# Fused two-block transformer pass: the first norm and its modulation as a pipeline over chunks, and the embedding product of the gated per-layer embedding ahead of its gate

## Chip, cores and metric

The kernel runs on one NeuronCore of a Trainium2 chip. The metric is the device time of one execution in microseconds (us), median over executions. Engines are named as the profile names them: PE (TensorE, matrix products; PEld its weight loads), DVE (VectorE), ACT (ScalarE), POOL (GpSimd), SP (SyncE, which issues nearly all DMAs).

## What is computed

A sequence of 512 tokens of width 1024 goes through two blocks. Only the places that the change touches are spelled out; the rest (differential attention, native sparse attention, two squared-ReLU MLPs, an mLSTM layer, a dilated window attention) is unchanged.

```python
# first block: conditioning by a vector c, layer 0
c_act = silu(c)                                      # (1, 1024)
mod = c_act @ ada_w[layer] + ada_b[layer]            # six rows of 1024
sh_a, sc_a, gt_a, sh_m, sc_m, gt_m = split(mod, 6)
h = rms_norm(x, attn_norm[layer]) * (1 + sc_a) + sh_a
mix = diff_attention(h, a_w_in, ...)                 # starts with h @ a_w_in (1024 x 3072)

# second block: per-layer embedding, once after the mLSTM layer, once at the very end
def ple_add(h, p_l, norm_g, w_gate, w_proj):
    gate = sigmoid(rms_norm_2(h, norm_g) @ w_gate)   # 1024 x 1024
    return h + (p_l @ w_proj) * gate                 # p_l: 512 x 256, w_proj: 256 x 1024
```

## The kernel before

Activations stand transposed in SBUF: `x` is 8 chunks (KC = 8) of 128 features by 512 tokens. All large weights come as one stream of halves of 128 x 2048 fp32 (1 MB) in the order of `STREAM`. Half n lands in slot n % 2 of `raw` (`load_half`, L600, issued by SP); ACT copies it rounded into `wH` (`hi`, L393), DVE writes the remainder `wL = raw - wH` (`lo`, L398). Activations are split in the same way into `hH` and `hL`. Each product of a 128 x 128 weight block with 512 tokens is three matmuls (`three`, L412 to L414). A tile of the output is four blocks of 128 rows in four PSUM banks and takes two halves and 96 matmuls (`tile_mm`); tile a uses banks 4 * (a % 2) onward.

A norm has three parts. `sq_act` (L485) squares the chunks, `sq_dve` (L493) adds the first seven up, `stats_pe` (L502, L505) multiplies by a matrix of 1/1024, which puts the mean on all partitions, and `rstd_act` (L509, L511) makes the inverse root. `apply_dve` and `apply_act` then make for each chunk the product tmp = x * scale * rstd (L515, DVE), hH (L549 or L551, ACT) and hL (L521 or L524, DVE).

Nothing is scheduled by a planner: each engine runs its own list (`act_first`, `dve_first`, ..., `pe_fourth`) in the order written, and semaphores tie them. An instruction that waits holds up all that stands behind it on its engine; this goes for SP's DMA issues too.

The first stage: SP loads c (broadcast), x, then 16 blocks of the modulation matrix as four transfers of 2 MB (`ada_h`), then halves 0 and 1 of the first weight, the relative-bias table `bt` (4 MB, by way of a row in DRAM) and, in the loop, one half and up to three further modulation blocks (`ada_load`, L593) a turn. DVE makes silu from ACT's exp(-c) with an addition, a reciprocal and a product (L1187 to L1191), adds up the squares, then takes the 16 dot products of modulation rows (`ada_sum`, L582: one pass over 128 x 1024 each), two small column operations (`mod_cols`, `mod_scale`), and applies the norm. PE runs the first tile after that.

The gated embedding (`ple_pe`, `ple_act`, `ple_dve`, L2297 to L2355): PE makes the two gate tiles (a, a + 1), then the product of the embedding with its weight (a + 2, a + 3), whose weight is a half of the stream, after them. ACT takes the sigmoid of the gate (L2308), DVE multiplies and adds to x (L2333, L2323). After the first use the next norm follows, after the second the output is stored (L2788). Before the last use, `dve_fourth` runs `lo` of the two first gate halves and only then the residual additions of the layer before (L2847 to L2850).

## Time and profile before

| | |
|---|---|
| median of 3 runs | 2163.93 us (2160.59 to 2164.48) |
| profiled execution | 2160.12 us, its span 2158.3 us |
| busy PE / PEld | 1986.0 us (92%) / 1634.8 us (76%) |
| busy DVE / ACT / POOL | 1173.3 us (54%) / 839.1 us (39%) / 0.2 us (0%) |
| mean granted TensorE clock | 0.953 of full speed |
| DMA | 223.85 MB, mean 104 GB/s |

The span runs from the first to the last instruction of the profiled execution. A row of the timeline gives start, length and engine, and in brackets how long the engine had been idle and what ended that. Lengths of matmuls overlap, since they are pipelined, so distances between starts are the better measure. A row of a window gives busy time and count of instructions for each engine, then the granted clock.

### The profile page before, as it was taken

The page shows a single profiled execution, that of the slowest core. Times are in us where ns is not written, and L with a number is a line of the kernel's source. Part 1 is how long each engine was busy: PE and PEld are TensorE (multiplying, and loading weights), DVE is VectorE, ACT ScalarE, POOL GpSimd, SP SyncE. Part 2 cuts the span into 40 slices and gives each one's busy share as a digit, 9 for nine tenths or more (in the row PEclk, how much of TensorE's full clock was granted, in tenths as well). Part 3 has the DMA queues.
Part 4 walks back from the last instruction along what each step waited for, and adds up shares of the span by engine and source line. Part 5 has one row for each costly group of instructions (what it writes and reads, how often), then busy time and mean ns, then how long its engine had stood idle before and what let it go on. Part 6 is the DMA issues. An engine that isn't in the chain of part 4 may idle for free.

```text
span 2158.3 us, 24312 instructions
## 1 busy us (share of the span) xinstructions
PE 1986.0 (92%) x9298; PEld 1634.8 (76%) x9298; DVE 1173.3 (54%) x2046; ACT 839.1 (39%) x1303; POOL 0.2 (0%) x4
## 2 busy tenths in 40 slices
PE   1999979999998998889899999997999999999969
PEld 0877658888886786889878888885878877777857
DVE  8557756565666375556544343436634554646553
ACT  3226624132233532356633132234344443556432
POOL 0000000000000000000000000000000000000000
PEclk9999999999999978699999999998999999999989
DMA  9551064565654221000022222221222132131021
GB/s 357 203 198 40 1 216 158 173 214 175 210 179 136 98 84 53 1 1 2 6 104 98 98 97 97 97 97 42 95 78 79 40 135 85 59 137 59 1 88 59
DMA packets 42216, 223.85 MB, mean 104 GB/s; under 512 B 4444, under 2 KB 5212, under 8 KB 23694
## 3 DMA queue, kind: packets, MB, share of 16 engines
q1 hardware_dynamic: 41602, 222.25, 29.4%
q8 instruction: 56, 0.92, 0.2%
q10 hardware_dynamic: 524, 0.41, 0.1%
q14 instruction: 34, 0.28, 0.0%
HBM read 219.45 MB, written 3.19 MB: 103 GB/s over the span
## 4 chain that ended last, share of the span: by engine, by line
PE 83%; DVE 8%; DMA 3%; ACT 3%; issue 2%; SPq 0%; DVEq 0%; ACTq 0%
PE bank L412 23%; PE bank L413 22%; PE bank L414 22%; PE bank L1487 3%; PE bank L1458 2%; DMA raw<-wts_d 1%; DMA adab<-ada_d 1%; PE bank L1448 1%; PE bank L2568 1%; PE bank L1449 1%; DMA ada<-ada_d 1%; DVE tmp L515 1%; ACT wH L393 1%; DVE wL L398 1%; PE bank L676 1%
## 5 line engine op out<-in xcount | busy, mean ns | idle before, releaser
L412 PE MATMUL bank<-hH,wH 128*128 128x512 f32 x1344 | 539.0, 401 | 68.2 <-DVE hL L524 36.9
L413 PE MATMUL bank<-hL,wH 128*128 128x512 f32 x1344 | 533.6, 397 | 0.0
L414 PE MATMUL bank<-hH,wL 128*128 128x512 f32 x1344 | 532.7, 396 | 0.0
L412 PEld LDWEIGHTS bank<-hH,wH 128*128 128x128 f32 x1344 | 258.9, 193 | 133.4 <-issue 70.1
L398 DVE TENSOR_TENSOR wL<-raw,wH 128x2048 fp32r<-128x2048 f32 x78 | 178.6, 2290 | 291.0 <-ACT wH L393 290.8
L941 ACT ACTIVATE wH<-raw 128x2048 fp32r<-128x2048 f32 x64 | 122.7, 1917 | 470.5 <-PE bank L414 470.5
L413 PEld LDWEIGHTS bank<-hL,wH 128*128 128x128 f32 x1344 | 259.1, 193 | 54.5 <-issue 1.0
L414 PEld LDWEIGHTS bank<-hH,wL 128*128 128x128 f32 x1344 | 258.5, 192 | 55.2
L393 ACT ACTIVATE wH<-raw 128x2048 fp32r<-128x2048 f32 x78 | 149.1, 1912 | 317.4 <-PE bank L414 281.7
L979 DVE TENSOR_TENSOR wL<-raw,wH 128x2048 fp32r<-128x2048 f32 x64 | 146.6, 2290 | 230.7 <-ACT wH L941 230.6
L414 PE MATMUL bank<-aH,wL 128*128 128x512 f32 x512 | 199.4, 389 | 0.0
L413 PE MATMUL bank<-aL,wH 128*128 128x512 f32 x512 | 199.4, 389 | 0.0
L412 PE MATMUL bank<-aH,wH 128*128 128x512 f32 x512 | 199.4, 389 | 0.0
L582 DVE CUSTOM_DVE_ANT_0 adab<-adab,cb 128x1024 f32<-128x1024 f32 x96 | 115.4, 1223 | 88.9 <-DMA adab<-ada_d 88.9
L412 PE MATMUL bank<-wH,hH 128*128 128x512 f32 x320 | 132.7, 415 | 2.4 <-ACT kT L1162 1.7
L414 PE MATMUL bank<-wH,hL 128*128 128x512 f32 x320 | 126.2, 394 | 0.0
L413 PE MATMUL bank<-wL,hH 128*128 128x512 f32 x320 | 126.1, 394 | 0.0
L412 PEld LDWEIGHTS bank<-aH,wH 128*128 128x128 f32 x512 | 96.1, 188 | 20.0
L414 PEld LDWEIGHTS bank<-aH,wL 128*128 128x128 f32 x512 | 96.1, 188 | 19.9
L413 PEld LDWEIGHTS bank<-aL,wH 128*128 128x128 f32 x512 | 96.1, 188 | 19.8
L1487 PEld LDWEIGHTS bank<-vB,ptB 128*128 128x128 f32 x640 | 90.3, 206 | 17.9 <-issue 5.7
L1549 DVE CUSTOM_DVE_ANT_0 sB<-bank,bt 128x128 f32<-128x128 f32 (+3 forms) x128 | 59.3, 488 | 75.8 <-PE bank L1449 75.1
(321 smaller groups left out, 2568.1 us busy)
## 6 DMA issues: line engine op xcount, KB each, us to landing
raw<-wts_d SPq DMA_DIRECT2D x142, 1024.0 KB, 4.9
adab<-ada_d SPq DMA_DIRECT2D x96, 512.0 KB, 4.3
ada<-ada_d SPq DMA_DIRECT2D x4, 2048.0 KB, 22.3
bt<-bias_rows SPq DMA_DIRECT2D x1, 4096.0 KB, 12.9
x<-x_d SPq DMA_DIRECT2D x1, 2048.0 KB, 9.6
out_d<-x SPq DMA_DIRECT2D x4, 512.0 KB, 2.7
pF<-p_d SPq DMA_DIRECT2D x2, 512.0 KB, 3.7
values_by_token<-vD SPq DMA_DIRECT2D x1, 1024.0 KB, 4.3
```

The lines of the kernel that those rows point to most:

```text
L393: act.activation(wH[:, n % 2, :], raw[:, n % 2, :], ACT.Copy).then_inc(w_hi, 1)
L398: dve.tensor_tensor(wL[:, n % 2, :], raw[:, n % 2, :], wH[:, n % 2, :].bitcast(F32), ALU.subtract).then_inc(w_lo, 1)
L412: pe.matmul(o, l[0], r[0], start=start, stop=False)
L413: pe.matmul(o, l[0], r[1], start=False, stop=False)
L414: return pe.matmul(o, l[1], r[0], start=False, stop=stop)
L515: dve.scalar_tensor_tensor(out=tmp[:, c % 3, :], in0=x[:, c, :], scalar=scale(c), in1=rstd[:, :], op0=ALU.mult, op1=ALU.mult).then_inc(tmp ...
L582: return dve.tensor_tensor_reduce(slot, slot, sb["cb"][:, :], 1.0, 0.0, ALU.mult, ALU.add, dst)
L941: act.activation(wH[:, n % 2, :], raw[:, n % 2, :], ACT.Copy).then_inc(w_hi, 1)
L979: dve.tensor_tensor(wL[:, n % 2, :], raw[:, n % 2, :], wH[:, n % 2, :].bitcast(F32), ALU.subtract).then_inc(w_lo, 1)
L1458: last = pe.transpose(bank[:, 2 + u % 2, j * P:(j + 1) * P], pB[:, u % 2, j * P:(j + 1) * P], ident[:, :])
L1487: last = pe.matmul(o[:, r * (HD + 1):(r + 1) * (HD + 1)], ptB[:, u % 2, part.start + j * P:part.start + (j + 1) * P], vB[:, j, b * GRP + g ...
L1549: dve.tensor_tensor_reduce(sB[:, u % 2, part], bank[:, u % 2, part], sb["bt"][:, 4 * g + r, T - w:T], -SCALE, BIG, ALU.add, ALU.min, nm[:, ...
```

## The change

First stage. ACT takes a sigmoid by table instead of the exponential and DVE multiplies it with c, so the addition and the reciprocal go; ACT loads one more table set after the sigmoid. The weight half 0 is loaded ahead of x. The 16 modulation blocks come as eight pairs (a shift block and its scale block, 1 MB) in four slots; a pair's two dot products start from the bias and gain columns, so that they give the finished shift and scale of one chunk. DVE makes for each chunk the two dot products and the norm's product, ACT writes hH and the shifted value, and POOL subtracts to hL. The table `bt` is no longer issued ahead of the loop over weight halves but in it, behind halves 2 to 4 and the modulation blocks 18 to 23, and half 5 stands behind it.

Gated embedding. Its weight leaves the stream and is loaded with p into the `bias` region (`peF`), split there (`ple_split_act`, `ple_split_dve`). PE makes chunks 0 and 1 of the product before the norm's statistics, 2 and 3 after them, 4 to 7 between the two gate tiles; ACT copies them to `pp`. The second gate tile comes last, its second half bank by bank. In the fourth part the residual additions now come ahead of `lo` of the first gate half, and `lo` of the second moves into the apply. After the first use three squares and sums of the next norm move.

```diff
         def sp_first(sp):
             sp.dma_start(sb["cb"][:, :], d["c"].to_broadcast([P, D])).then_inc(cb_back, 16)
+            load_half(sp, 0)
             sp.dma_start(x[:, :, :], d["x"]).then_inc(x_in, 16)
-            for g in range(4):
...
+            for c in range(KC):
+                if c >= 4:
+                    sp.wait_ge(ada_pre, 2 * (c - 4) + 2)
+                sp.dma_start(ada_pair(c), pairs[c]).then_inc(ada_h[c % 4], 16)
+                if c == 2:
                     load_half(sp, 1)
...
+            load_half(sp, 2)
+            for k in range(2):
+                ada_load(sp, 16 + k)
             sp.wait_ge(f_row, 2)
             sp.dma_start(fscr, sb["frow"][:, :]).then_inc(f_out, 16)
...
-            for n in range(12):
+            for n in range(1, 12):
                 load_half(sp, n + 2)
-                for k in range(max(3 * n - 1, 0), min(3 * n + 2, 24)):
+                for k in range(3 * n - 1, min(3 * n + 2, 24)):
                     ada_load(sp, 16 + k)
+                if n == 2:
+                    sp.wait_ge(f_out, 16)
+                    sp.dma_start(sb["bt"][:, :, :], skewed).then_inc(bt_in, 16)
...
-            act.activation(sb["ce"][:, :], sb["cb"][:, :], ACT.Exp, scale=-1.0).then_inc(first_e, 1)
+            act.activation(sb["ce"][:, :], sb["cb"][:, :], ACT.Sigmoid).then_inc(first_e, 1)
+            act.preload_act_table_set(EXP_LN)
...
-            apply_act(act, 0, lambda c: mod(c))
+            for c in range(KC):
+                act.wait_ge(tmp_done, c + 1)
+                t = tmp[:, c % 3, :]
+                act.activation(hH[:, c, :], t, ACT.Identity, bias=mod(c))
+                act.activation(t, t, ACT.Identity, bias=mod(c)).then_inc(h_hi, 1)
+                if c == 1:
+                    hi(act, 1)
...
+            def pair_sums(c):
+                dve.wait_ge(ada_h[c % 4], 16 * (c // 4 + 1))
+                a = ada_pair(c)
+                dve.tensor_tensor_reduce(a[:, 0, :], a[:, 0, :], cb, 1.0, col("ada_b", c), ALU.mult, ALU.add,
+                                         mod(c)).then_inc(ada_pre, 1)
+                dve.tensor_tensor_reduce(a[:, 1, :], a[:, 1, :], cb, col("attn_norm", c), start[:, c:c + 1],
+                                         ALU.mult, ALU.add, mod(8 + c)).then_inc(ada_pre, 1)
...
+            for c in range(KC):
+                pair_sums(c)
+                dve.wait_ge(ada_pre, 2 * c + 2)
+                if c == 0:
+                    dve.wait_ge(rstd_done, 1)
+                if c >= 3:
+                    dve.wait_ge(h_lo, c - 2)
+                dve.scalar_tensor_tensor(out=tmp[:, c % 3, :], in0=x[:, c, :], scalar=mod(8 + c), in1=rstd[:, :],
+                                         op0=ALU.mult, op1=ALU.mult).then_inc(tmp_done, 1)
+                if c == 2:
+                    lo(dve, 1)
...
+        @block.gpsimd
+        def _(pool):
+            for c in range(KC):
+                pool.wait_ge(h_hi, c + 1)
+                pool.tensor_tensor(hL[:, c, :], tmp[:, c % 3, :], hH[:, c, :].bitcast(F32), ALU.subtract)\
+                    .then_inc(h_lo, 1)
...
         def ple_act(act, l, a, n):
             act.preload_act_table_set("sigmoid_and_others")
+            ple_product_act(act, l, a, 0)
+            hi(act, n + 2)
+            act.wait_ge(half_used, n + 2)
+            for m in range(4):
+                o, freed = evac(act, a + 2, m)
+                act.activation(sg[:, m, :], o, ACT.Sigmoid).then_inc(freed, 1)
+            ple_product_act(act, l, a, 1)
+            hi(act, n + 3)
+            if n + 4 < N_HALF:
+                hi(act, n + 4)
+            for m in range(4):
+                o, freed = evac(act, a + 3, m)
+                bank_done(act, DONE0[a + 3], m, n + 4)
+                act.activation(sg[:, 4 + m, :], o, ACT.Sigmoid).then_inc(freed, 1)
+                if l == 0 and m < 3:
+                    sq_act(act, 7, lambda e, c: e.wait_ge(ple_x, c + 1), [m])
+            if n + 4 < N_HALF:
+                act.preload_act_table_set(EXP_LN)
...
+            for c in range(4, KC):
+                gated(c)
+                if l == 0 and 5 <= c:
+                    sq_dve(dve, 7, [c - 4])
+                grow(c)
...
         def dve_fourth(dve):
+            sq_dve(dve, 7, range(4, 7))
...
             d_dve(dve)
-            lo(dve, N_DO + 2)
-            lo(dve, N_DO + 3)
+            ple_split_dve(dve, 1)
             dve.wait_ge(half_used, N_DO + 1)
             residual_dve(dve, 67, 0, None)
+            lo(dve, N_DO + 2)
             sq_dve(dve, 8, [1, 2, 3])
             second_tile(dve, 8, 68, None, N_DO + 2)
-            apply_dve(dve, 9, 8, lambda c: col("ple_norm", 8 + c), None)
+            apply_dve(dve, 9, 8, lambda c: col("ple_norm", 8 + c), None, lambda e: lo(e, N_DO + 3))
             ple_dve(dve, 1, 69, N_G1)
...
             last.then_inc(half_used, 1)
+            ple_product_pe(pe, 1, 69, (0, 1))
             stats_pe(pe, 8, 69)
+            ple_product_pe(pe, 1, 69, (2, 3))
             ple_pe(pe, 1, 69, N_G1, 72)
```

The order on DVE in the first stage, after the sums of squares: `ada_62` is the buffer of modulation blocks, the dot product is an `ISA` row with its accumulator read behind it. Before, from the last blocks to the norm's products:

```order
L582 ISA ada_63,mods<-ada_63,cb 128x1024
L582 ISA mods 128x1
L398 TENSOR_TENSOR wL<-raw,wH 128x2048
L1079 TENSOR_TENSOR mods<-mods,cols 128x16
L1086 SCALAR_TENSOR_TENSOR mods<-mods,cols 128x8
L515 SCALAR_TENSOR_TENSOR tmp<-x,mods,rstd 128x512 x3
L524 SCALAR_TENSOR_TENSOR hL<-tmp,mods,hH 128x512
```

and in the changed kernel, chunks 0 and 1:

```order
L496 TENSOR_TENSOR tmp<-tmp 128x512 x6
L1223 ISA ada_62,mods<-ada_62,cb,cols 128x1024
L1223 ISA mods 128x1
L1225 ISA ada_62,mods<-ada_62,cb,rs,cols 128x1024
L1225 ISA mods 128x1
L1236 SCALAR_TENSOR_TENSOR tmp<-x,mods,rstd 128x512
L1223 ISA ada_62,mods<-ada_62,cb,cols 128x1024
```

The norm's product stands behind two dot products instead of sixteen, and the rows for hL are gone from DVE.

The order on DVE in the fourth part, from the last row of the attention on. Before:

```order
L2694 TENSOR_TENSOR hL<-qD,hH 128x512
L398 TENSOR_TENSOR wL<-raw,wH 128x2048 x2
L574 TENSOR_TENSOR x<-bank,x 128x512 x4
L493 TENSOR_TENSOR tmp<-tmp 128x512 x3
L574 TENSOR_TENSOR x<-bank,x 128x512 x2
```

and in the changed kernel:

```order
L2776 TENSOR_TENSOR hL<-qD,hH 128x512
L2335 TENSOR_TENSOR pL<-pF,pH 128x1024
L2337 TENSOR_TENSOR peL<-peF,peH 128x2048
L577 TENSOR_TENSOR x<-bank,x 128x512 x4
L401 TENSOR_TENSOR wL<-raw,wH 128x2048
L496 TENSOR_TENSOR tmp<-tmp 128x512 x3
L577 TENSOR_TENSOR x<-bank,x 128x512 x2
```

The four residual additions stand behind the two splits of the embedding instead of behind two weight splits.

## Rows read from the trace of the kernel before

**Rows 1.** Timeline of PE, first stage: start, us, [idle before it <- who ended that]

```profile
20.00 2.05 PE L502 MATMUL bank<-tmp,mean 128*128 128x512 f32 x2 [20.00 <-DVE tmp L493]
...
49.85 0.77 PE L412 MATMUL bank<-hH,wH 128*128 128x512 f32 x1 [23.86 <-DVE hL L524]
```

**Rows 2.** The chain that ended last, first stage: start, us

```profile
22.19 13.42 DMA raw<-wts_d
```

**Rows 3.** Timeline of DVE, first stage

```profile
15.19 4.67 DVE L493 TENSOR_TENSOR tmp<-tmp 128x512 f32<-128x512 f32 x6
...
20.91 1.22 DVE L582 CUSTOM_DVE_ANT_0 ada<-ada,cb 128x1024 f32<-128x1024 f32 x1
...
22.06 1.22 DVE L582 CUSTOM_DVE_ANT_0 ada<-ada,cb 128x1024 f32<-128x1024 f32 x1
...
37.57 2.29 DVE L398 TENSOR_TENSOR wL<-raw,wH 128x2048 fp32r<-128x2048 f32 x1 [3.00 <-ACT wH L393]
...
46.97 2.08 DVE L515 SCALAR_TENSOR_TENSOR tmp<-x,mods,rstd 128x512 f32<-128x512 f32 x3
```

**Rows 4.** Timeline of ACT, first stage

```profile
10.75 1.67 ACT L485 ACTIVATE tmp<-x 128x512 f32<-128x512 f32 x3 [4.17 <-DMA x<-x_d]
...
23.79 0.69 ACT L509 ACTIVATE rstd<-bank,one 128x512 f32<-128x512 f32 x1 [4.01 <-PE bank L505]
...
50.53 0.72 ACT L551 ACTIVATE hH<-tmp,mods 128x512 fp32r<-128x512 f32 x1 [0.73 <-DVE tmp L515]
```

**Rows 5.** DMA issues, 0 to 120 us: KB each, median us to landing

```profile
bt<-bias_rows SPq DMA_DIRECT2D x1, 4096.0 KB, 12.9
```

**Rows 6.** DMA issues, 2060 to 2100 us

```profile
raw<-wts_d SPq DMA_DIRECT2D x2, 1024.0 KB, 4.9
```

**Rows 7.** Timeline of ACT: the first instruction after the fourth tile

```profile
138.62 2.06 ACT L1162 ACTIVATE kT<-bank 128x512 f32<-128x512 f32 x4 [8.90 <-PE bank L414]
```

**Rows 8.** Timeline of PE around the first gated embedding

```profile
1762.71 1.02 PE L502 MATMUL bank<-tmp,mean 128*128 128x512 f32 x2
...
1769.69 0.70 PE L412 MATMUL bank<-hH,wH 128*128 128x512 f32 x1 [4.25 <-DVE hL L521]
...
1827.96 1.10 PE L502 MATMUL bank<-tmp,mean 128*128 128x512 f32 x2 [2.01 <-DVE tmp L493]
...
1837.16 0.47 PE L412 MATMUL bank<-hH,wH 128*128 128x512 f32 x1 [4.25 <-DVE hL L521]
```

**Rows 9.** Timeline of ACT after the first gated embedding

```profile
1819.05 1.28 ACT L2310 ACT_TABLE_LOAD   x1
```

**Rows 10.** Windows: length, busy of PE, PEld, DVE, ACT, POOL, then granted clock

```profile
2096.70:2100.50 3.80, 3.79 (x9) 3.03 (x10) 3.73 (x6) 1.60 (x3) 0.00 (x0) 0.50 0.00 0
2100.50:2104.00 3.50, 3.50 (x16) 2.84 (x16) 3.43 (x6) 1.97 (x4) 0.00 (x0) 0.95 0.02 5
```

**Rows 11.** Timeline of SP, DVE and PE ahead of the last gated embedding

```profile
2058.10 0.33 SPq L2784 DMA_DIRECT2D pF<-p_d  x1
...
2077.70 2.29 DVE L398 TENSOR_TENSOR wL<-raw,wH 128x2048 fp32r<-128x2048 f32 x1 [8.58 <-ACT wH L393]
2079.91 2.48 DVE L574 TENSOR_TENSOR x<-bank,x 128x512 f32<-128x512 f32 x4
...
2088.71 2.04 PE L502 MATMUL bank<-tmp,mean 128*128 128x512 f32 x2 [13.05 <-DVE tmp L493]
2090.55 1.92 PE L505 MATMUL bank<-tmp,mean 128*128 128x512 f32 x2
...
2096.71 0.77 PE L412 MATMUL bank<-hH,wH 128*128 128x512 f32 x1 [4.24 <-DVE hL L521]
```

**Rows 12.** The end: last matmul, sigmoids, last additions, stores

```profile
2142.47 2.07 ACT L2308 ACTIVATE sg<-bank 128x512 f32<-128x512 f32 x4 [8.90 <-PE bank L414]
2152.92 0.39 PE L414 MATMUL bank<-pH,wL 128*128 128x512 f32 x1
2153.95 1.28 DVE L2323 TENSOR_TENSOR x<-x,sg 128x512 f32<-128x512 f32 x2
```

More of the change, by code:

```diff
@@ L308, in place @@
     t("sg", [P, KC, T], "hid")
+    t("pp", [P, KC, T], "hid", 16 * K)
+    t("peF", [P, HALF], "bias")
+    t("peH", [P, HALF], "bias", 8 * K, F32R)
+    t("peL", [P, HALF], "bias", 16 * K, F32R)
     t("pF", [P, 2, T], "misc")
@@ L466, in program @@
         sq_sum = sem("sq_sum")
-        SUMMED = [4 if s == 7 else 7 for s in range(9)]
+        SUMMED = [7] * 9
         SUM0 = [sum(SUMMED[:s]) - s for s in range(9)]
@@ new lines, in dve_first @@
+            start = rs[:, 16:24]
+            dve.scalar_tensor_tensor(out=start, in0=cols[:, COL0["ada_b"] + 8:COL0["ada_b"] + 16], scalar=1.0,
+                                     in1=cols[:, COL0["attn_norm"]:COL0["attn_norm"] + KC], op0=ALU.add,
+                                     op1=ALU.mult).then_inc(cb_ready, 1)
+            dve.wait_ge(first_e, 2)
+            dve.tensor_tensor(one[:, 2:3], cc[:, 0, 3:4], cc[:, 0, 2:3], ALU.subtract).then_inc(lam_s, 1)
+            dve.wait_ge(lam_s, 3)
@@ L2290, in m_core_dve, with ple_load @@
                 rest(c, c - 4)
[L2293 to L2295 removed]
+        p_in, p_hi, p_lo, ple_x, ple_mm, ple_g = (sem(n) for n in (
+            "p_in", "p_hi", "p_lo", "ple_x", "ple_mm", "ple_g"))
+        sg, pF, pH, pL, pp = (sb[n] for n in ("sg", "pF", "pH", "pL", "pp"))
+        peF, peH, peL = sb["peF"], sb["peH"], sb["peL"]
+        def ple_load(sp, l):
+            sp.dma_start(pF[:, :, :], d["p"][l]).then_inc(p_in, 16)
+            sp.dma_start(peF[:, :], d["ple"][l]).then_inc(p_in, 16)
@@ new lines, in ple_split_act, with ple_split_dve @@
+        def ple_split_act(act, l):
+            act.wait_ge(p_in, 32 * (l + 1))
+            act.activation(pH[:, :, :], pF[:, :, :], ACT.Copy).then_inc(p_hi, 1)
+            act.activation(peH[:, :], peF[:, :], ACT.Copy).then_inc(p_hi, 1)
+        def ple_split_dve(dve, l):
+            dve.wait_ge(p_hi, 2 * l + 1)
+            dve.tensor_tensor(pL[:, :, :], pF[:, :, :], pH[:, :, :].bitcast(F32), ALU.subtract).then_inc(p_lo, 1)
+            dve.wait_ge(p_hi, 2 * l + 2)
+            dve.tensor_tensor(peL[:, :], peF[:, :], peH[:, :].bitcast(F32), ALU.subtract).then_inc(p_lo, 1)
@@ new lines, in ple_product_pe @@
+        def ple_product_pe(pe, l, a, chunks):
+            pe.wait_ge(p_lo, 2 * l + 2)
+            for c in chunks:
+                if c < 4:
+                    pe.wait_ge(acc_free[0], 4 * ((a - 1) // 2) + c + 1)
+                else:
+                    pe.wait_ge(acc_free[1], 4 * (a // 2) + c - 4 + 1)
+                for k in range(2):
+                    w = slice(k * D + c * P, k * D + (c + 1) * P)
+                    last = three(pe, bank[:, c % 4, :], (peH[:, w], peL[:, w]), (pH[:, k, :], pL[:, k, :]),
+                                 k == 0, k == 1)
+                last.then_inc(ple_mm, 1)
@@ L2309, in ple_act @@
-            if n + 6 < N_HALF:
+            ple_product_act(act, l, a, 0)
[8 more added lines that the diff above has]
+                hi(act, n + 4)
+            for m in range(4):
+                o, freed = evac(act, a + 3, m)
[3 more added lines that the diff above has]
+                    sq_act(act, 7, lambda e, c: e.wait_ge(ple_x, c + 1), [m])
@@ L2338, in ple_dve @@
[L2338 to L2355 removed]
+            lo(dve, n + 2)
@@ new lines, in ple_dve, with block @@
+            gated(0)
+            for c in range(1, 4):
+                gated(c)
+                grow(c - 1)
+            grow(3)
+            lo(dve, n + 3)
+            if n + 4 < N_HALF:
+                lo(dve, n + 4)
+            for c in range(4, KC):
+                gated(c)
+                if l == 0 and 5 <= c:
+                    sq_dve(dve, 7, [c - 4])
+                grow(c)
+        def ple_pe(pe, l, a, n, hbase):
+            def block(t, j, kk, m):
+                k = 4 * j + kk
+                return three(pe, bank[:, 4 * (1 - t) + m, :], wpart((n + 2 * t + j) % 2, kk, m * P, P),
+                             (hH[:, k, :], hL[:, k, :]), k == 0, k == KC - 1)
+            acc_wait(pe, a)
+            for j in range(2):
+                pe.wait_ge(w_lo, n + j + 1)
+                for kk in range(4):
+                    pe.wait_ge(h_lo, hbase + 4 * j + kk + 1)
+                    for m in range(4):
+                        last = block(0, j, kk, m)
+                last.then_inc(half_used, 1)
+            ple_product_pe(pe, l, a, range(4, KC))
+            pe.wait_ge(w_lo, n + 3)
+            for kk in range(4):
+                for m in range(4):
+                    if kk == 0:
+                        pe.wait_ge(acc_free[0], 4 * ((a + 1) // 2) + m + 1)
+                    last = block(1, 0, kk, m)
+            last.then_inc(half_used, 1)
+            pe.wait_ge(w_lo, n + 4)
+            for m in range(4):
+                for kk in range(4):
+                    last = block(1, 1, kk, m)
+                last.then_inc(m_done if m < 3 else half_used, 1)
```

161 lines of the change are left out of this document (50 added, 111 removed).

## Prediction

> **What bounds the kernel now.** PE is busy for 92% of the span, so time can come only from stretches in which it stands still, or from work taken off it. I read first what PE waits for at the start: 20.0 us for the sums of squares and 23.86 us for the first hL, so that its first tile begins at 49.85 [rows 1]. The chain that ended last tells what is behind the second wait: a transfer, the first weight half, queued behind 8 MB of modulation blocks and landed at 35.6 us [rows 2]. The timelines of DVE and ACT give the prices, the DMA issues those of transfers, and PE's rows around the two gated embeddings show three more gaps: 4.25 us ahead of the first gate, 2.0 and 4.25 us after it [rows 8], and 13.05 and 4.24 us ahead of the last [rows 11].
>
> **Prices.** A matmul at full clock starts every 0.22 to 0.23 us (16 in 3.5 us), at the lower level of 1.2 GHz 9 take 3.8 us [rows 10]. I use 0.227: 2.72 us for the 12 matmuls of one chunk, 10.9 for a half, 21.8 for a tile, 1.36 for one chunk of the embedding product (6). A spell at the low level ahead of a tile costs 3.8 - 9 x 0.227 = 1.8 us. A dot product takes 1.15 us (22.06 - 20.91), `lo` 2.2 with the hand-over, ACT's rounding ahead of it 1.9 (landed at 35.6 [rows 2], `lo` begins at 37.57), a norm's product 2.08 / 3 = 0.69 [rows 3], hH 0.7 [rows 4]. 4 MB land 12.9 us after issue [rows 5], 1 MB 4.9 us [rows 6]: 2.67 us for each MB and 2.2 us fixed.
>
> **Start, up to the first tile.** The silu by table saves nothing by itself: the squares wait for x, landed at 10.75 [rows 4], and the dot products for their blocks. Half 0 ahead of x costs 1 MB, so x lands at 13.4 and the six sums, which took from 15.2 to 19.9 since DVE was still at the silu, now run from about 15.0 to 19.5. The statistics and the root take what they took (19.9 to 25.2: Ln begins at 23.8 and takes 0.69, the Exp after it as much [rows 4]), so rstd is there at 24.7. Pair 0 (4.5 MB in all) lands at about 16 and is summed by 22. From 24.7 DVE sets the pace: per chunk 2 x 1.15 + 0.69 + 0.1 for semaphores = 3.1 us, above PE's 2.72. With `lo` of half 1 and its wait (2.5) the eighth product ends at 24.7 + 0.7 + 7 x 3.1 + 2.5 = 49.6. Pairs 4 to 7 are issued when their slots come free; the last, at about 35, lands at 40 and is wanted at 46, so they are hidden. hH and the shifted value take 1.4 us.
>
> The subtraction on POOL has no row. Its nearest row is the same operation on DVE, 0.6 to 0.7 us, from below; from above I take the DVE price of a subtraction four times as wide, 2.29 us. I take 1.2, nearer the lower end, since the operation and size are those of the lower row and only the engine differs. Then the last chunk is ready at 49.6 + 1.4 + 1.2 = 52.2 and the tile ends at 54.9. It ended at 49.85 + 21.8 + 1.4 (its first matmuls were slow) = 73.0: **18.1 us** less.
>
> **What is late next.** Tile 1 wants `lo` of half 2, behind the eighth apply: 49.6 + 1.4 + 1.9 (ACT) + 2.2 = 55.1, 0.2 us lost. Then the queue. `bt` went out before PE had begun; now SP issues it after modulation block 23, which waits for the sum of block 21, at about 70 us (54.9 and from there two halves' turns on DVE, each `lo` and three dot products whose blocks come 3.5 us after their slots are free). Half 5 is issued behind it: (4 + 1) x 2.67 + 2.2 = 15.6 us, landing at 86; block 24, next in the queue, at 87.6. On DVE the sum of block 24 stands ahead of `lo` of half 5: 87.6 + 1.15 + 2.2 = 91.1. PE wants it at 55.1 + 3 x 10.9 = 87.8. I count a **new wait of 3.3 us**. Bounds: 0, if the queue lets the small transfers through, and 6 with a slower `bt`. From there the loop has its old slack. The fourth tile, which ended at 138.5 [rows 7], ends at 55.1 + 65.3 + 3.3 = 123.7. **Start: -14.8 us.**
>
> **First gated embedding.** Chunks 0 and 1 of the product, 2.7 us, stand ahead of the statistics, which began at 1762.71 with no gap [rows 8]. A part of these 2.7 us was a wait for the eighth square, so statistics end 1.95 us later; the gate starts at 1771.6 instead of 1769.7. Chunks 2 and 3 lie in the 4.25 us gap. With only 1.7 us of it left I expect no spell at the low clock: -1.8 us (bounds 0 and -1.8). Chunks 4 to 7 cost 5.4 us between the tiles. The second tile ends at 1771.6 + 21.8 + 5.4 + 21.8 = 1820.6; before, the product ended at 1825.8. What follows is worse than before: ACT has the last sigmoid (0.5 us), a table load (1.28) [rows 9] and only then square 3, and DVE's `sq_dve` of chunk 3 stands ahead of the last addition to x. Counting on at 0.64 us a step (1.28 / 2) [rows 12] (square 3, sum 3, addition, then sums 4 to 6, each fed by a square) the sum is complete 6.1 us after the tile's end, and PE, idle so long, makes the statistics at the low clock in 3.8 us (2088.71 to 2090.55 + 1.9) [rows 11] instead of about 2. The next tile starts 4.25 us later, at 1820.6 + 6.1 + 3.8 + 4.25 = 1834.8 against 1837.16: **-2.4 us** (bounds -0.6 and -4.2 by the two clock terms). The splits added ahead of that (1.2 + 2.3 us on DVE) stand with four residual additions (2.5 us) [rows 11] in front of `lo` of a half that PE wants 10.9 us before 1762.7, at 1751.8: its slot is free at 1740.9, and 1740.9 + 2.5 + 3.5 + 2.2 = 1749.1. They cost nothing, with 2.7 us of cover.
>
> **Last gated embedding.** The 13 us gap came from `lo` of the second gate half (2077.7), which had to wait for PE to free its slot and stood ahead of the residual additions (2079.9) [rows 11]. Now DVE has ahead of them only the splits. p is issued at 2058.1; with its weight behind it, 1.5 MB, they land at 2058.1 + 0.4 + 4.0 + 2.2 = 2064.4 or so. ACT (1.9) rounds the weight by 2066.3, DVE is through with the remainder at 2068.6. The additions and sums took 8.7 us from 2079.9 to the start of the statistics; with one `lo` (2.2) among them: 2068.6 + 8.7 + 2.2 = 2079.5 instead of 2088.7, 9.2 us. Chunks 0 and 1 of the product fill PE's wait, so it stays warm and the statistics take 2.1 instead of 3.8 us, another 1.7; the gate starts at 2079.5 + 2.1 + 4.24 = 2085.8, 10.9 us earlier, and without the slow spell (1.8). Chunks 0 to 3 lie in gaps: 5.4 us less behind the gate. The end is a sigmoid longer: 0.5 + 0.69 + 0.68 with the hand-overs, 2.3 us after the last matmul against 2.1 [rows 12]. **-10.9 - 1.8 - 5.4 + 0.2 = -17.9 us**; without the clock term -16.1.
>
> **Sum.** -14.8 - 2.4 - 17.9 = -35.1 us. The profiled execution took 2160.12 us and would take 2125.0. The median, 2163.93, is 3.8 us above it, and gives 2128.8. I forecast 2128.8 for the median.
>
> **Rivals.**
> 1. *POOL's subtraction holds DVE up.* It becomes ready while DVE is in the second dot product; if the two engines exclude each other, POOL starts at its end and the norm's product, on the path, waits for it: its length less 0.1 us, seven times. With 1.2 us: +7.7, **2136.5**; with 0.69 and 2.29: +4 and +15. For it: DVE is the bottleneck there and its rows are back to back. Against it: no row shows POOL and DVE together at all. The Trainium skill states just this rule (SBUF — State Buffer, "Who interferes with whom"): a DVE instruction with two SBUF inputs and a GpSimd instruction that reads SBUF lock each other out of a shared read interface for the whole instruction. No run here shows it yet. The skill's GPSIMD Engine Reference (3.1) has a two-input operation on GpSimd 1.96 times as long as on VectorE, which would make an estimate of 1.35 us of the 0.69 row, and with it the lock would cost 8.8 us.
> 2. *`bt` hides.* If queue and loop have more slack than I count, the 3.3 us are not lost: **2125.5**.
> 3. *The embedding's weight is late.* In the fourth part everything I gain begins with peL at 2068.6. If the 1 MB lands 10 us late, the 9.2 us go: **2138.0**. Against it: DMA moves little there.
> 4. *Slower than before: POOL sets the pace.* The product of chunk c waits for hL of chunk c - 3. Once a subtraction takes more than 3.1 us the chain runs at POOL's pace and the tile ends near 29.5 + 8 x its length. The other parts bring 20.3 us and the waits behind the tile take 3.5, so against 73.0 the total turns positive at a tile end of 89.8, a subtraction of 7.5 us; at 8.5 us it ends at 97.5 and the time is **2171.6**. That is nearly four times my upper row.
> 5. *Nothing moves:* the gaps close but the waits turn up again one stage later, 2164. The stages after the first tiles are bound by PE, which speaks against it.
>
> **How the numbers follow.** Forecast 0.47, rival 1 0.33, rival 2 0.10, rival 3 0.05, rival 4 0.02, rival 5 0.03. The forecast's own range is 2121 to 2133: 3.8 us for where the median falls, 3.6 for the two clock terms of 1.8. With rivals 1 to 3 and the middle of the bounds of POOL the range is 2119 to 2142. A measurement of this kernel tells about 0.2%, 4.3 us, from no change: faster 0.95, same 0.03, slower 0.02.
>
> **What would show it.** Right: first hL product on PE near 28 us, DVE's norm products 3.1 us apart, the fourth tile's evacuation near 124 us with one PE wait for `lo` of about 4 us behind `bt`; PE's longest wait ahead of the last gate about 1 us; the last matmul 2.3 us ahead of the last addition. Rival 1 shows in DVE's rows about 4.2 us apart, with POOL's rows in the holes. Wrong would be: a wait of PE above 5 us in the fourth part, a POOL row above 3 us, or waits for weights in tiles 1 and 2.

## Result and profile after

| | before | after |
|---|---|---|
| median | 2164.2 us (2160.59 to 2164.86, 4 runs) | 2149.43 us (2146.22 to 2151.21, 4 runs) |
| profiled execution, its span | 2160.12 us, 2158.3 us | 2151.21 us, 2149.4 us |
| busy PE / DVE / ACT / POOL | 1986.0 / 1173.3 / 839.1 / 0.2 us | 1991.0 / 1169.8 / 853.0 / 16.3 us |
| mean granted TensorE clock | 0.953 | 0.946 |

The ratio is 0.9933, 95% interval 0.9916 to 0.9951: 14.8 us faster by the medians, faster by more than the 0.2% that can be told. The forecast was 2128.8 us with a range of 2119 to 2142: too low by 20.6 us, and the measured time lies above the range. The two profiled executions lie at opposite ends of their sets (before's is its fastest, after's its slowest), so their spans differ by 8.9 us only. I therefore read the traces stage by stage, each against a landmark just ahead of it, and come back at the end to what lies between the stretches.

| stretch | before | after | forecast | measured |
|---|---|---|---|---|
| span's start to the fourth tile's evacuation (ACT, kT) | 138.62 | 140.39 | -14.8 | **+1.8** |
| ACT's table load ahead of the second m_out tile, to the first product of kv2 | 1726.95 to 1837.16: 110.21 | 1733.47 to 1843.55: 110.08 | -2.4 | **-0.1** |
| issue of `pF` for the last embedding, to the span's end | 2058.10 to 2158.3: 100.2 | 2066.21 to 2149.4: 83.2 | -17.9 | **-17.0** |

The page's busy line of the changed kernel:

```profile
PE 1991.0 (93%) x9292; PEld 1635.7 (76%) x9292; DVE 1169.8 (54%) x2038; ACT 853.0 (40%) x1328; POOL 16.3 (1%) x12
```

Most of the miss, 16.6 us, is in the table's first row. PE's first tile begins at 34.52 us, 15.3 us earlier than in [rows 1], where 28 was forecast:

```profile
25.06 2.04 PE L505 MATMUL bank<-tmp,mean 128*128 128x512 f32 x2 [25.06 <-DVE tmp L496]
...
34.52 0.77 PE L415 MATMUL bank<-hH,wH 128*128 128x512 f32 x1 [4.81 <-POOL hL L3004]
```

DVE's timeline of the first stage after the change (rows as in [rows 3]):

```profile
6.69 1.23 DVE L1201 TENSOR_TENSOR cb<-cb,ce 128x1024 f32<-128x1024 f32 x1 [5.39 <-ACT ce L1147]
15.60 0.22 DVE L1205 CUSTOM_DVE_ANT_0 lamb<-lamb 128x64 f32<-128x64 f32 x1 [7.68 <-DMA lamb<-lam_d]
...
18.04 2.29 DVE L401 TENSOR_TENSOR wL<-raw,wH 128x2048 fp32r<-128x2048 f32 x1 [1.39 <-ACT wH L396]
20.25 4.66 DVE L496 TENSOR_TENSOR tmp<-tmp 128x512 f32<-128x512 f32 x6
...
30.04 0.75 DVE L1236 SCALAR_TENSOR_TENSOR tmp<-x,mods,rstd 128x512 f32<-128x512 f32 x1 [2.65 <-ACT rstd L514]
30.71 1.28 DVE L1223 CUSTOM_DVE_ANT_0 ada<-ada,cb,cols 128x1024 f32<-128x1024 f32 x1
...
31.91 1.34 DVE L1225 CUSTOM_DVE_ANT_0 ada<-ada,cb,rs 128x1024 f32<-128x1024 f32 x1
...
33.30 1.62 DVE L1236 SCALAR_TENSOR_TENSOR tmp<-x,mods,rstd 128x512 f32<-128x512 f32 x1
34.84 1.27 DVE L1223 CUSTOM_DVE_ANT_0 ada<-ada,cb,cols 128x1024 f32<-128x1024 f32 x1
...
36.05 1.33 DVE L1225 CUSTOM_DVE_ANT_0 ada<-ada,cb,rs 128x1024 f32<-128x1024 f32 x1
...
37.43 1.65 DVE L1236 SCALAR_TENSOR_TENSOR tmp<-x,mods,rstd 128x512 f32<-128x512 f32 x1
...
41.20 2.30 DVE L1223 CUSTOM_DVE_ANT_0 ada<-ada,cb,cols 128x1024 f32<-128x1024 f32 x1
...
44.81 0.75 DVE L1236 SCALAR_TENSOR_TENSOR tmp<-x,mods,rstd 128x512 f32<-128x512 f32 x1
...
60.50 1.63 DVE L1236 SCALAR_TENSOR_TENSOR tmp<-x,mods,rstd 128x512 f32<-128x512 f32 x1
```

Two things are to be seen. DVE stood still for 7.68 us, until 15.60. Its wait is for all five small transfers of ACT's queue, and the profile names the broadcast lambda rows (`lamb`) as the last to land. The sums of squares began at 20.25 instead of the forecast 15.0 and the first product at 30.04 instead of 24.7. And the products are 4.13 us apart (33.30 to 37.43), not 3.1: six of the eight show 1.62 to 1.66 us, but the first and the fourth (44.81), which have no POOL work beside them, 0.75. Ahead of the fourth, the dot product at 41.20 has POOL's third subtraction (40.52 to 42.41) beside it and takes 2.30 us where the others take 1.28. POOL's timeline of the same stretch:

```profile
32.24 2.14 POOL L3004 TENSOR_TENSOR hL<-tmp,hH 128x512 fp32r<-128x512 f32 x1 [31.79 <-ACT tmp L1163]
36.37 2.16 POOL L3004 TENSOR_TENSOR hL<-tmp,hH 128x512 fp32r<-128x512 f32 x1 [1.99 <-ACT tmp L1163]
...
63.57 1.29 POOL L3004 TENSOR_TENSOR hL<-tmp,hH 128x512 fp32r<-128x512 f32 x1 [2.00 <-ACT tmp L1163]
```

The last subtraction, with DVE idle beside it, takes 1.29 us; the others 1.89 to 2.17. The second row shows what happens. It starts at 36.37 while DVE's dot product runs (36.05 to 37.38) and ends at 38.53, which is the dot product's end plus 1.15; DVE's product starts at 37.43 and ends 0.55 us after POOL. Each waits for the other inside its own row.

The third place is the third tile, which takes the weight halves 4 and 5 (counted from zero it is tile 2; the expectation of `bt_early` below calls it tile 1). SP's timeline and the DMA issues (KB, median us to landing; 12.9 in [rows 5]), then the timelines of DVE and PE, then windows (length; busy PE, PEld, DVE, ACT, POOL; granted clock), all of the changed kernel:

```profile
82.58 0.43 SPq L1128 DMA_DIRECT2D bt<-bias_rows  x1
83.06 4.83 SPq L603 DMA_DIRECT2D raw<-wts_d  x1
```

```profile
bt<-bias_rows SPq DMA_DIRECT2D x1, 4096.0 KB, 15.2
```

```profile
101.59 1.23 DVE L585 CUSTOM_DVE_ANT_0 adab<-adab,cb 128x1024 f32<-128x1024 f32 x1 [14.48 <-DMA adab<-ada_d]
...
102.74 2.28 DVE L401 TENSOR_TENSOR wL<-raw,wH 128x2048 fp32r<-128x2048 f32 x1
```

```profile
105.08 0.79 PE L415 MATMUL bank<-hH,wH 128*128 128x512 f32 x1 [4.46 <-DVE wL L401]
```

```profile
98.00:102.00 4.00, 2.62 (x12) 1.84 (x10) 0.41 (x1) 1.67 (x1) 0.00 (x0) 1.00 0.75 301
102.00:106.00 4.00, 0.92 (x2) 0.83 (x3) 4.00 (x4) 2.19 (x5) 0.00 (x0) 0.65 0.55 184
106.00:110.00 4.00, 4.00 (x11) 3.03 (x11) 1.40 (x4) 1.17 (x1) 0.00 (x0) 0.50 0.98 381
```

On DVE the `lo` of half 5 stands behind the dot product of a modulation block that landed only at 101.6 us, 19.0 us after the issue of `bt`. PE waits 4.46 us, and then the granted clock is at 0.50, the 1.2 GHz level, with 11 matmuls in 4 us. The forecast had the wait, at 3.3 us, and no low clock behind it.

Ahead of the first embedding PE waited for a weight half (first row below); behind it the statistics took 3.7 us, the low-clock length, as forecast:

```profile
1749.36 0.47 PE L415 MATMUL bank<-hH,wH 128*128 128x512 f32 x1 [2.00 <-DVE wL L401]
...
1835.56 2.05 PE L505 MATMUL bank<-tmp,mean 128*128 128x512 f32 x2 [6.24 <-DVE tmp L496]
1837.40 1.92 PE L508 MATMUL bank<-tmp,mean 128*128 128x512 f32 x2
1843.55 0.76 PE L415 MATMUL bank<-hH,wH 128*128 128x512 f32 x1 [4.24 <-DVE hL L524]
```

PE around the last embedding, beside [rows 11], with the waits of 13.05 and 4.24 us down to 1.20, 0.40 and 1.49:

```profile
2084.99 0.47 PE L415 MATMUL bank<-pH,peH 128*128 128x512 f32 x1 [1.20 <-DVE x L577]
...
2088.37 1.10 PE L505 MATMUL bank<-tmp,mean 128*128 128x512 f32 x2 [0.40 <-DVE tmp L496]
...
2094.91 0.47 PE L415 MATMUL bank<-hH,wH 128*128 128x512 f32 x1 [1.49 <-DVE hL L524]
```

### The profile page after: what moved, and what is told of

Read it like the earlier page. It is cut to its first block, busy times and chain, and to the rows that moved or that the text cites. A ratio compares the mean times of both kernels' runs of the same rounds, so it can differ in the third digit from the quotient of the medians.

```text
span 2149.4 us, 24339 instructions
## 1 busy us (share of the span) xinstructions
PE 1991.0 (93%) x9292; PEld 1635.7 (76%) x9292; DVE 1169.8 (54%) x2038; ACT 853.0 (40%) x1328; POOL 16.3 (1%) x12
## 4 chain that ended last, share of the span: by engine, by line
PE 80%; DVE 9%; DMA 4%; ACT 3%; issue 2%; SPq 0%; ACTq 0%; DVEq 0%
PE bank L415 21%; PE bank L416 21%; PE bank L417 21%; PE bank L1511 3%; DMA adab<-ada_d 2%; PE bank L1482 2%; DVE wL L401 1%; PE bank L1472 1%; DVE tmp L496 1%; PE bank L2650 1%; DVE adab L585 1%; DMA raw<-wts_d 1%; PE bank L1473 1%; ACT wH L396 1%; PE bank L679 1%
## 5 line engine op out<-in xcount | busy, mean ns | idle before, releaser
L401 DVE TENSOR_TENSOR wL<-raw,wH 128x2048 fp32r<-128x2048 f32 x76 | 173.9, 2289 | 226.6 <-ACT wH L396 226.3
L982 DVE TENSOR_TENSOR wL<-raw,wH 128x2048 fp32r<-128x2048 f32 x64 | 146.5, 2289 | 227.8 <-ACT wH L944 227.8
```

The lines of the kernel that those rows point to most:

```text
L401: dve.tensor_tensor(wL[:, n % 2, :], raw[:, n % 2, :], wH[:, n % 2, :].bitcast(F32), ALU.subtract).then_inc(w_lo, 1)
L982: dve.tensor_tensor(wL[:, n % 2, :], raw[:, n % 2, :], wH[:, n % 2, :].bitcast(F32), ALU.subtract).then_inc(w_lo, 1)
```

## Experiments

Five costs were suspected: T1, DVE's wait for `lamb` (5.2 us); T2, POOL and DVE excluding each other (six products longer by 0.87 and one dot product by 1.02, 6 us); T3, `bt` ahead of half 5 (4.46 us and a low clock); T4, the embedding's weight ahead of a weight half (2.0 us); T5, a table load and a sum of squares ahead of the last addition of the first embedding (2.1 us). Against all of them stood one thought: that the loss was elsewhere, or that removing one wait only lengthens the next. Before took 2163 to 2165 us as a median in every comparison.

### The two parts alone

`ple_only` has the start of the kernel before and the new gated embeddings; `start_only` the reverse. Each leaves the other part's lines of the diff out, for example in `ple_only`:

```diff
-                act.activation(hH[:, c, :], t, ACT.Identity, bias=mod(c))
-                act.activation(t, t, ACT.Identity, bias=mod(c)).then_inc(h_hi, 1)
...
+            apply_act(act, 0, lambda c: mod(c))
...
```

> Start of the kernel before, gated embeddings of the changed kernel. Theory A (parts are independent; the start gained nothing, the embeddings gave 2.1 and 17.0 us and the weight half behind the projection cost 2.0): 17 us below before, 2147 us (2144 to 2150), so as fast as the whole change or 2 us faster; DVE's last addition 19 us ahead of PE's end as seen from the second embedding's first issue is unchanged from the whole change: last matmul 2.3 us ahead of the last addition. Rival B (the start did bring its 14.8 us and the embeddings gave back as much): 2162 us or more.

> Start of the changed kernel, gated embeddings of the kernel before. Theory A (the start is worth nothing as built): ACT's fourth tile ends at 139 to 141 us of the span (138.6 before), time 2163 to 2168 us, no change that can be measured. Rival B (the start brings its 14.8 us and something behind it gives them back in the whole change): the fourth tile ends near 124 us and the time is near 2149 us.

`ple_only`: 2145.51 us (6 runs), ratio 0.9925 (0.9911 to 0.9939). Its stretches are those of the whole change: 110.11 us around the first embedding (1724.80 to 1834.91), 83.3 us at the end (2057.71 to 2141.0). `start_only`: 2164.05 us (12 runs), ratio 1.0002 (0.9989 to 1.0015); its fourth tile is evacuated at 139.99, its end takes 100.1 us. The parts are independent: the start as built is worth nothing that can be measured, and the whole gain of the change is that of the embeddings. ACT's row of the fourth tile in `start_only`, beside [rows 7]:

```profile
139.99 2.06 ACT L1172 ACTIVATE kT<-bank 128x512 f32<-128x512 f32 x4 [8.90 <-PE bank L413]
```

### T1: lambda off the front

```diff
-                    act.dma_start(dst, d[name]).then_inc(par_in, 16)
+                    act.dma_start(dst, d[name]).then_inc(par2_in if name == "cols" else par_in, 16)
...
-            act.wait_ge(lam_s, 2)
-            act.activation(cc[:, 0, 2:4], cc[:, 0, 0:2], ACT.Exp).then_inc(first_e, 1)
             hi(act, 0)
             sq_act(act, 0, xw_loaded, range(KC))
             rstd_act(act, 0, 0)
+            act.wait_ge(lam_s, 2)
+            act.activation(cc[:, 0, 2:4], cc[:, 0, 0:2], ACT.Exp).then_inc(first_e, 1)
...
-            dve.wait_ge(par_in, 80)
+            dve.wait_ge(par2_in, 16)
...
```

> The changed kernel, but VectorE waits only for the column table ahead of its work; the lambda rows, their two dot products and their exponential come behind the sums of squares, the rest of lambda behind the eighth norm product. Theory T1 (VectorE's wait for the broadcast lambda rows, until 15.6 us, holds up everything behind it): the first norm product starts at 24.5 to 25.5 us instead of 30.0, every chunk 5 us earlier, the fourth tile ends near 135 us instead of 140.4, time 2144 us (2141 to 2147). Rival (the tiles behind the first are paced by transfers: bias table and weight halves): the first product is earlier all the same, but tile 1 waits longer, the fourth tile stays within 1.5 us of 140.4, time 2148 to 2151 us.

Measured 2142.71 us (5 runs), ratio 0.9906 (0.9893 to 0.9920), 6.7 us under the changed kernel by the medians. DVE's timeline of `lam_late`:

```profile
10.49 2.29 DVE L401 TENSOR_TENSOR wL<-raw,wH 128x2048 fp32r<-128x2048 f32 x1 [2.54 <-ACT wH L396]
15.24 4.67 DVE L496 TENSOR_TENSOR tmp<-tmp 128x512 f32<-128x512 f32 x6 [2.46 <-ACT tmp L488]
...
25.32 0.75 DVE L1231 SCALAR_TENSOR_TENSOR tmp<-x,mods,rstd 128x512 f32<-128x512 f32 x1 [2.64 <-ACT rstd L514]
```

The sums begin at 15.24 (forecast 15.0), the first product 4.7 us earlier, and the fourth tile is evacuated at 136.14, 4.25 us earlier. T1 holds. PE's wait behind `bt` is 4.71 us, against 4.46: the wait passed the gain on. Of the 6.7 us by the medians only these 4.25 have a row; the rest is within the spread of the executions.

### T3: the bias table into the idle stretch

```diff
                 load_half(sp, n + 2)
+                if n == 1:
+                    sp.wait_ge(f_out, 16)
+                    sp.dma_start(sb["bt"][:, :, :], skewed).then_inc(bt_in, 16)
                 for k in range(3 * n - 1, min(3 * n + 2, 24)):
                     ada_load(sp, 16 + k)
-                if n == 2:
-                    sp.wait_ge(f_out, 16)
-                    sp.dma_start(sb["bt"][:, :, :], skewed).then_inc(bt_in, 16)
```

> The changed kernel with the bias table's transfer issued right behind weight half 3 (n = 1 in place of n = 2), into the stretch in which the queues are idle. Theory T3 (the bias table ahead of weight half 5 costs PE 4.5 us of waiting in tile 1 and 2.5 us of low clock behind it): that wait falls under 1 us, tiles 1 to 3 run without it, the fourth tile ends at 133 to 136 us instead of 140.4, time 2143 us (2140 to 2147). Rival (the modulation rows or another half take the place of the bias table as the last to land, and the wait moves or stays): PE's waits for the low half in tiles 1 to 3 still sum to 4 us or more and the time is 2147 to 2151 us.

Measured 2142.2 us (5 runs), ratio 0.9903 (0.9890 to 0.9916). `bt` goes out at 56.82 instead of 82.58, into a stretch (57 to 69 us) in which the DMA engines of the changed kernel were busy for 4% of the time at most. PE's waits from 60 to 142 us (waited for: us in total, times, longest), first of the changed kernel, then of `bt_early`:

```profile
PE bank L415 <- DVE wL L401: 4.5, 1, 4.5
PE bank L415 <- POOL hL L3004: 1.4, 2, 1.1
```

```profile
PE bank L415 <- ACT kT L1176: 1.7, 1, 1.7
PE bank L415 <- POOL hL L3004: 1.4, 2, 1.1
PE bank L415 <- DVE wL L401: 1.1, 1, 1.1
```

and the windows of `bt_early` in the place of those above:

```profile
102.00:106.00 4.00, 4.00 (x20) 3.30 (x19) 3.05 (x2) 0.92 (x1) 0.00 (x0) 1.00 0.86 297
106.00:110.00 4.00, 4.00 (x19) 3.34 (x18) 1.53 (x4) 0.00 (x0) 0.00 (x0) 1.00 0.84 253
```

The wait of 4.5 us is gone, 39 matmuls run in the eight microseconds in which 13 had run, and the fourth tile is evacuated at 133.58, 6.8 us earlier. T3 holds, and prices `bt`'s place at 6.8 us: 4.46 of waiting, the other 2.3 at the low clock behind it (11 matmuls from 105.08 to 109.94, 4.86 us instead of the 2.5 that they take at 0.227). Two of the waits listed lie behind the fourth tile: the 1.7 us for kT, which the kernel before has too (140.74), and the 1.1 us for `wL` (139.83), which is new, so some of the 6.8 us is lost again there.

### T1 and T3 together

Both edits above in one kernel.

> The late lambda and the early bias table together. Theory (two separate costs, both on the way of the first four tiles): first norm product at 25.3 us, fourth tile ends at 140.4 - 4.3 - 6.8 = 129.3 us (128 to 131), time 2136 us (2133 to 2139). Rival (they share one cost: with the first tile 5 us earlier, weight half 4 or the bias table comes too late again): the fourth tile ends at 132 us or later, time over 2139 us.

Measured 2136.16 us (4 runs), ratio 0.9886 (0.9864 to 0.9908). The fourth tile is evacuated at 128.49, 11.9 us earlier than in the changed kernel (4.25 + 6.8 = 11.05 from the two alone). The costs are separate; the 0.85 us above their sum has no explanation here.

### T2: who reads beside whom

Both start from `lam_bt`. `low_on_dve` takes POOL out, and with it ACT's second pass over each chunk; `low_memset` keeps POOL and every wait, but gives it an operation that reads nothing and leaves the low part of the first norm out of the result:

```diff
-                act.activation(hH[:, c, :], t, ACT.Identity, bias=mod(c))
-                act.activation(t, t, ACT.Identity, bias=mod(c)).then_inc(h_hi, 1)
+                act.activation(hH[:, c, :], tmp[:, c % 3, :], ACT.Identity, bias=mod(c)).then_inc(h_hi, 1)
...
+                dve.scalar_tensor_tensor(out=hL[:, c, :], in0=tmp[:, c % 3, :], scalar=mod(c),
+                                         in1=hH[:, c, :].bitcast(F32), op0=ALU.add,
+                                         op1=ALU.subtract).then_inc(h_lo, 1)
```

```diff
-                pool.tensor_tensor(hL[:, c, :], tmp[:, c % 3, :], hH[:, c, :].bitcast(F32), ALU.subtract)\
+                pool.memset(hL[:, c, :].bitcast(F32), 0.0)\
```

> As lam_bt, but the low part hL of the first norm is made by VectorE from product, shift and high part (one operation per chunk), ScalarE writes the high part alone, GpSimd does nothing. Theory T2 (GpSimd's subtraction and VectorE's two-input operations exclude each other, as the products' 1.62 us beside 0.75 us suggest): all eight products take 0.75 us, a chunk costs VectorE 2.5 + 0.1 + 0.67 + 0.7 = 4.0 us instead of 4.14, the last low part is ready 3 us earlier, the fourth tile ends 1 to 3 us earlier than in lam_bt, time 1 to 3 us under lam_bt. Rival (the 1.62 us are a wait for the slot in tmp that ScalarE and GpSimd still hold, in a chain of three slots): products still show over 1.2 us, the pace grows to 4.9 us by the added operation and the fourth tile ends 3 to 6 us later than in lam_bt.

> As lam_bt, but GpSimd fills hL of the first norm with zeros in place of subtracting: the low part of the first norm's result is left out, everything else and all waits stay. Theory T2 (exclusion by GpSimd's reads): products take 0.75 us, the pair sums behind them 2.5 us, pace 3.3 us instead of 4.14, eighth product's start 5.5 us earlier than in lam_bt (near 50.4), tile 0 ends near 55 us, the fourth tile 4 to 5.5 us earlier than in lam_bt. Rival (the wait for a slot of tmp): a slot is freed by GpSimd's operation as before, so products still show over 1.2 us and the pace stays over 3.8 us.

DVE's second, third and last product in `low_memset`, with the dot product between the first two of them:

```profile
28.49 0.75 DVE L1231 SCALAR_TENSOR_TENSOR tmp<-x,mods,rstd 128x512 f32<-128x512 f32 x1
...
30.36 1.34 DVE L1215 CUSTOM_DVE_ANT_0 ada<-ada,cb,rs 128x1024 f32<-128x1024 f32 x1
...
31.75 0.75 DVE L1231 SCALAR_TENSOR_TENSOR tmp<-x,mods,rstd 128x512 f32<-128x512 f32 x1
...
50.27 0.75 DVE L1231 SCALAR_TENSOR_TENSOR tmp<-x,mods,rstd 128x512 f32<-128x512 f32 x1
```

and POOL's row beside that dot product:

```profile
30.66 0.53 POOL L3004 MEMSET hL<- 128x512 f32 x1 [2.73 <-ACT tmp L1163]
```

All eight products take 0.75 us and are 3.26 us apart, `lo` of half 1 aside; the eighth starts at 50.27 (55.71 in `lam_bt`) and the fourth tile is evacuated at 122.88, 5.6 us earlier. POOL's row begins and ends inside the dot product, and neither is lengthened: POOL's write beside DVE's reads costs nothing here, where the subtraction of the changed kernel ended only 1.15 us behind such a dot product. The rival was a wait for a slot of `tmp`. The zeros take 0.53 us instead of 1.29, so they free a slot sooner, and `low_memset` by itself would not refute it. The changed kernel does: only the products of chunk 3 and later wait for a slot (`if c >= 3`), yet those of chunks 1 and 2 take 1.62 and 1.65 us, and that of chunk 3, which has the wait, takes 0.75. What held DVE was POOL's reading. In `low_on_dve` the products take 0.75 us too, and the low parts on DVE, 0.74 us each, give back most of it: 3.92 us per chunk. The fourth tile is evacuated at 126.96, 1.5 us earlier than in `lam_bt`, with 2132.23 us (4 runs), ratio 0.9856 (0.9836 to 0.9876). By the medians that is 3.9 us under `lam_bt`, more than the 1 to 3 expected; the four executions of `lam_bt` lie 10 us apart (2131.23 to 2141.34), so I hold to the rows. So a subtraction that POOL took off DVE saved DVE 0.66 us (3.92 - 3.26) and cost it 0.87 us (1.62 - 0.75). `low_memset` took 2130.48 us (4 runs).

### T4 and T5: the first embedding

```diff
+                load_half(sp, n)
                 if n == N_MO + 2:
                     sp.wait_ge(y_lo, 16 + 8)
                     ple_load(sp, 0)
...
-                load_half(sp, n)
...
-                    sq_act(act, 7, lambda e, c: e.wait_ge(ple_x, c + 1), [m])
-            if n + 4 < N_HALF:
-                act.preload_act_table_set(EXP_LN)
+                    sq_act(act, 7, lambda e, c: e.wait_ge(ple_x, c + 1), [m] if m < 2 else [2, 3])
...
-            sq_act(act, 7, lambda e, c: e.wait_ge(ple_x, c + 1), range(3, KC))
+            sq_act(act, 7, lambda e, c: e.wait_ge(ple_x, c + 1), range(4, 7))
+            act.preload_act_table_set(EXP_LN)
+            sq_act(act, 7, lambda e, c: e.wait_ge(ple_x, c + 1), [7])
...
-                if l == 0 and 5 <= c:
+                if l == 0 and c in (5, 6):
                     sq_dve(dve, 7, [c - 4])
                 grow(c)
+                if l == 0 and c == 6:
+                    sq_dve(dve, 7, [3])
```

> The changed kernel with two places of the first gated embedding altered: weight half N_MO + 2 is issued ahead of pF and peF (not behind them), and the table load stands between the squares of chunks 6 and 7, with the square and sum of chunk 3 ahead of the last gate's chunk. Theory T4: PE's 2.0 us wait for the low weight half in the second m_out tile goes. Theory T5: VectorE's last sum of squares ends 2.1 us earlier behind the last sigmoid (4.0 us after that sigmoid's start, not 6.0). Together 4 us: 2145.4 us (2143 to 2148). Rival (one of the two is hidden behind something else: the projection's low part lands later and PE waits for it ahead of the statistics, or the row sums of the statistics are held by ScalarE): each shows in its own rows, time 2147 to 2150 us.

Measured 2142.09 us (4 runs), ratio 0.9906 (0.9888 to 0.9925). PE's rows behind the embedding, to be set beside those of the changed kernel:

```profile
1827.46 2.04 PE L505 MATMUL bank<-tmp,mean 128*128 128x512 f32 x2 [4.50 <-DVE tmp L496]
1829.29 1.91 PE L508 MATMUL bank<-tmp,mean 128*128 128x512 f32 x2
1835.45 0.76 PE L415 MATMUL bank<-hH,wH 128*128 128x512 f32 x1 [4.24 <-DVE hL L524]
```

From the table load (1729.40) to this last row 106.05 us pass instead of 110.08, the 4 us expected: PE has no wait for a weight half left there, and the wait behind the last sigmoid is 4.50 instead of 6.24 us. T4 and T5 hold, with T5 at 1.7 us by that row. The median lies below the 2143 to 2148 expected: it differs from the changed kernel's by 7.3 us, 3.3 more than the stretch. In the two profiled executions 4.1 us had already come about ahead of it (1733.47 against 1729.40), in code that is the same, and I do not count them. Another 1.2 us come behind it, from the first product of kv2 to the issue of `pF` (221.44 us against 222.66); more of that stretch below.

### All of it together

> All that the earlier runs showed to cost: late lambda, early bias table, low part of the first norm on VectorE, weight half ahead of the projection, table load between the last squares. Theory (the costs are separate and add): the fourth tile ends at 127.0 us as in low_on_dve, the stretch from the table load ahead of the second m_out tile to the first product of kv2 takes 106.0 us as in emb_mend (110.1 in the changed kernel), time 2132.2 - 4 = 2128 us (2124 to 2131), below both kernels and below the forecast that the changed kernel missed. Rival (the gains overlap: an earlier start meets a low clock or a transfer later on): 2132 us or more, with both stretches as said but the difference lost between them.

Measured 2128.94 us (2128.11 to 2130.66, 5 runs), ratio 0.984 (0.9825 to 0.9856). ACT's fourth tile, then PE's first product of kv2, 106.06 us behind the table load at 1717.56:

```profile
126.91 2.07 ACT L1174 ACTIVATE kT<-bank 128x512 f32<-128x512 f32 x4 [8.90 <-PE bank L417]
```

```profile
1823.62 0.76 PE L415 MATMUL bank<-hH,wH 128*128 128x512 f32 x1 [4.24 <-DVE hL L524]
```

The costs add. This version is 20.5 us faster than the changed kernel and 35.9 us faster than the one before (2164.81 in its comparison).

## Why the prediction was wrong

**Right.** The last embedding: -17.9 forecast, -17.0 measured, step by step from the issue of `pF`. The weight's low part was forecast 10.5 us behind it and took 11.2 (2066.21 to 2077.4), the statistics 21.4 against 22.2, the gate 27.7 against 28.7, with PE warm; PE's longest wait ahead of the gate was to be about 1 us and is 1.49. The first embedding by itself: -2.4 forecast; -0.1 measured with a wait of 2.0 us in it that was forecast at nothing, so -2.1 without it.

**Wrong: "the six sums ... now run from about 15.0 to 19.5".** They ran from 20.25. The step priced the landing of x and of the blocks, and put at nothing the wait for the parameters, which the change moves on DVE's queue from behind three quarters of the dot products to the front; ACT's exponential of lambda moved with it, ahead of `hi` of half 0. `lamb` had landed by 15.60 us. The trace of before could not show when: DVE read it there only at 33.5 us, and PE's matmul behind the same wait began at 23.68, both without waiting. Price: 5.3 us at the first product; taken away, 4.7 us there and 4.25 us at the fourth tile.

**Wrong: "= 3.1 us, above PE's 2.72".** It is 4.14 wherever POOL subtracts beside DVE, as rival 1 had it (4.2). The forecast was preferred to this rival because no row showed POOL and DVE together, which is no evidence either way, while DVE as the bottleneck spoke for the rival. The Trainium skill (SBUF — State Buffer, "Who interferes with whom") stated the mutual exclusion, and the traces agree: POOL's subtraction, which reads, lengthens DVE's product from 0.75 to 1.62 us, and in `low_memset` the operation that only writes lengthens nothing. The operation's length, taken as 1.2 us, is 1.29; the estimate by the Trainium skill's GPSIMD Engine Reference (3.1) was 1.35. The eighth low part was ready at 64.86 us (63.57 + 1.29) where 52.2 had been forecast: 12.7 late, 5.3 of it lambda's. The other 7.4 are, to 0.1 us, the lock and the dot products: 6.3 for six products longer by 0.87 to 0.91 and one dot product longer by 1.02, and 1.2 for dot products that take 1.21 and 1.26 us from start to start where 1.15 had been taken seven times over. With POOL's reads taken away the fourth tile ends 5.6 us earlier. Rival 1 had the mechanism, but its 2136.5 is still 12.9 us short, since it knew nothing of lambda and of the low clock behind `bt`.

**Mis-sized: "a new wait of 3.3 us".** The wait was 4.46 us and was followed by the low clock; moving `bt` gave 6.8 us, so the term is short by 3.5 us. The mechanism, half 5 and the modulation row behind `bt`, was right. The term's own sum has a slip: 70 + 15.6 + 1.3 for the half megabyte of block 24 is 86.9 and not 87.6, so that it should have read 2.5 us. And the list of signs calls waits for weights in tiles 1 and 2 wrong, while the forecast's own wait falls in tile 2. The forecast left out that the clock may fall behind a wait in the middle of a tile, though it priced such a spell at the embeddings.

**Wrong: "they cost nothing, with 2.7 us of cover".** That cover belonged to another half. The step counted DVE's and ACT's new splits ahead of `lo` of half N_MO + 3, and not the new 1 MB in SP's queue ahead of half N_MO + 2, for which PE waited 2.00 us.

The three terms of the start, 5.3 + 7.4 + 3.5 = 16.2, make up nearly all of the 16.6 us by which its forecast failed. With lambda and `bt` mended and POOL reading nothing the fourth tile ended at 122.88 us. That this is near the 123.7 forecast is in part luck: the forecast contains a wait of 3.3 us that this version doesn't have, and prices POOL's operation at 1.2 us where the zeros take 0.53, so like for like it stays some 3 us late.

With 2.3 us of the first embedding and 0.9 of the last the three stretches miss their forecasts by 19.8 us, and the medians by 20.3 (35.1 - 14.8). This agreement is partly luck too, since the two traces also differ between the stretches. From the fourth tile to the table load the changed kernel took 4.8 us longer (1593.1 against 1588.3). Over all eleven traces that stretch lies between 1584.7 (`lam_bt`) and 1594.3 us (`bt_early`) and follows no edit, so I take it for spread. From the first product of kv2 to the issue of `pF` it took 1.7 us longer, and here the traces do follow an edit: 220.94 and 220.84 us with the old embeddings (before and `start_only`), 222.6 to 222.9 in the seven kernels with the new ones as built, 221.4 in `emb_mend` and `all_mended`. PE's work there is the same. Its granted clock was 0.50 from 2023.55 to 2029.55 us in the changed kernel and 0.72 in the corresponding 2017.16 to 2023.16 before. So most of the 2.1 us credited to the first embedding went again behind it, a cost that the prediction left out; why the clock differs was not tested.
